# A three-block fp32 network on one core: the end of a stage and the start of the next run by token tile

## What is computed

```python
for i in range(2):                      # blocks 0 and 1
    g = norm_g[i]
    h = h + 0.5 * rmsnorm(swiglu(rmsnorm(h, g[0]), wg1[i], wu1[i], wd1[i]), g[1])
    u = rmsnorm(h, g[2])
    m = diff_attention(u) if i == 0 else neighborhood_attention(u)   # w_in 1024x3072, w_out 1024x1024
    h = h + rmsnorm(m, g[3])
    h = h + 0.5 * rmsnorm(swiglu(rmsnorm(h, g[4]), wg2[i], wu2[i], wd2[i]), g[5])
def swiglu(x, wg, wu, wd):              # wg, wu 1024x2816, wd 2816x1024
    return (silu(x @ wg) * (x @ wu)) @ wd
# third block
p = rmsnorm(h, ga) @ w_in               # two attentions of 8 heads, forget logits, 2048 gate columns
h = h + (gates[0] * (o_a @ w_branch_moba) + gates[1] * (o_b @ w_branch_fox)) @ w_out
u, g = split(rmsnorm(h, gf) @ w_ffn_up)
out = h + (silu(causal_conv3(g)) * u) @ w_ffn_down
```

## Time and profile before

| | before |
|---|---|
| median of 3 runs | 1442.16 us (1442.08 to 1443.78) |
| the profiled execution | 1442.12 us, span 1440.3 us |
| PE busy | 1422.6 us |
| DVE, ACT, POOL busy | 858.5, 747.9, 90.9 us |
| granted PE clock, whole span | 1.00 |
| transfers | 248.21 MB, mean 172 GB/s |

### The profile page before, as it was taken

One profiled execution on the slowest core, in us unless ns is written; L12 is line 12 of the kernel. 1 busy time (PEld: TensorE's weight loads), 2 busy tenths in 40 slices (PEclk: granted clock), 3 DMA queues, 4 the chain that ended last, 5 costly groups with the idle time before them and its releaser, 6 DMA issues.

```text
span 1440.3 us, 20791 instructions
## 1 busy us (share of the span) xinstructions
PE 1422.6 (99%) x6864; PEld 1184.1 (82%) x6864; DVE 858.5 (60%) x1113; ACT 747.9 (52%) x1216; POOL 90.9 (6%) x115
## 2 busy tenths in 40 slices
PE   9999999999999999999999999999999999999999
PEld 7888888778888888888888988888888898888887
DVE  5555575767555565555655665555657756565654
ACT  6444464656444454444546654444545465465553
POOL 2110110012111000000100000000013000000000
PEclk9999999999999999999999999999999999999999
DMA  9877746315655656556463155566565513555551
GB/s 304 245 224 219 219 155 210 118 59 160 190 189 189 203 162 190 189 187 195 157 219 111 37 160 189 188 187 201 181 208 161 176 60 104 178 167 181 184 183 53
DMA packets 189938, 248.21 MB, mean 172 GB/s; under 512 B 15194, under 2 KB 128101, under 8 KB 189760
## 3 DMA queue, kind: packets, MB, share of 16 engines
q1 hardware_dynamic: 187904, 241.35, 53.1%
q0 software_dynamic: 1984, 6.21, 1.9%
HBM read 246.33 MB, written 1.17 MB: 172 GB/s over the span
## 4 chain that ended last, share of the span: by engine, by line
PE 93%; DVE 3%; ACT 1%; issue 1%; POOL 1%; DMA 0%; SPq 0%; ACTq 0%; DVEq 0%; POOLq 0%
PE ps L272 26%; PE ps L274 26%; PE ps L273 26%; PE ps L760 2%; PE ps L796 2%; PE ps L555 1%; PE ps L785 1%; PE ps L285 1%; DVE h L476 1%; PE ps L367 1%; PE ps L962 1%; PE ps L286 1%; PE ps L290 1%; PE ps L332 1%; PE ps L331 1%
## 5 line engine op out<-in xcount | busy, mean ns | idle before, releaser
L265 DVE TENSOR_TENSOR wlo<-raw,whi 128x1024 fp32r<-128x1024 f32 x450 | 549.5, 1230 | 393.4 <-ACT whi L257 393.2
L257 ACT CAST whi<-raw 128x1024 fp32r<-128x1024 f32 x450 | 469.9, 1051 | 361.5 <-PE ps L274 344.9
L272 PE MATMUL ps<-whi,xhi 128*128 128x512 f32 x1280 | 499.9, 391 | 0.0
L274 PE MATMUL ps<-whi,xlo 128*128 128x512 f32 x1280 | 498.2, 389 | 0.0
L273 PE MATMUL ps<-wlo,xhi 128*128 128x512 f32 x1280 | 498.0, 389 | 0.0
L274 PEld LDWEIGHTS ps<-whi,xlo 128*128 128x128 f32 x1280 | 240.2, 188 | 50.3
L272 PEld LDWEIGHTS ps<-whi,xhi 128*128 128x128 f32 x1280 | 240.3, 188 | 49.5
L273 PEld LDWEIGHTS ps<-wlo,xhi 128*128 128x128 f32 x1280 | 240.3, 188 | 49.3
L272 PE MATMUL ps<-whi,thi 128*128 128x512 f32 x400 | 160.5, 401 | 0.0
L274 PE MATMUL ps<-whi,tlo 128*128 128x512 f32 x400 | 156.4, 391 | 0.0
L273 PE MATMUL ps<-wlo,thi 128*128 128x512 f32 x400 | 156.0, 390 | 0.0
(11 more groups left out here) (181 smaller groups left out, 1141.2 us busy)
## 6 DMA issues: line engine op xcount, KB each, us to landing
raw<-in_ffn_wg_dram SPq DMA_DIRECT2D x176, 256.0 KB, 2.9
raw<-in_ffn_wu_dram SPq DMA_DIRECT2D x176, 256.0 KB, 3.1
raw<-in_ffn_wd_dram SPq DMA_DIRECT2D x176, 256.0 KB, 3.0
raw<-in_w_ffn_up_dram SPq DMA_DIRECT2D x88, 256.0 KB, 3.5
raw<-in_w_in_dram SPq DMA_DIRECT2D x80, 256.0 KB, 3.3
raw<-in_diff_w_in_dram SPq DMA_DIRECT2D x48, 256.0 KB, 3.0
raw<-in_na_w_in_dram SPq DMA_DIRECT2D x48, 256.0 KB, 3.1
raw<-in_w_ffn_down_dram SPq DMA_DIRECT2D x44, 256.0 KB, 3.0
```

Of the source, the lines that this page charges most:

```text
L257: nc.scalar.copy(whi[:, s], raw[:, s]).then_inc(s_hi, 1)
L265: nc.vector.tensor_tensor(wlo[:, s], raw[:, s], whi[:, s].bitcast(F32), ALU.subtract).then_inc(s_lo, 1)
L272: nc.tensor.matmul(outs[t], ahi[:, c], whi[:, s, i], start=start, stop=False)
L274: last = nc.tensor.matmul(outs[t], alo[:, c], whi[:, s, i], start=False, stop=stop)
```

## The change

Three things. **The end:** the last three units of f0 to f3, out0 and out1 (the last two of out2) run through `held_rows`, all tile-0 products of the held units first, then tile 1; ahead of the last unit's tile-1 products stand the first four transposes of the next stage. The turned hidden of an FFN's last chunk goes to `xhi`/`xlo` (k 6 and 7), so that it doesn't wait for unit n0+63. The end of f4 stays as it was. **The start:** `first_chunk` works the first four units of the next stage as tile 0 rounded products, tile 0 residual products (`xlo`), tile 1, with the other twelve transposes of h between them, four at a time; `keep_warm` is gone there. ACT and DVE split the turned h in pieces of 128 x 128 (`split_act`, `split_dve`), 16 on each instead of 8 of 128 x 256. The chunk writes banks Y and Y+1. **The kernel's start** has the same form, with x in three transfers between the units, and the gains on ACT's queue.

```diff
+        def rounded_part(pe, n0, r, j, t):
+            s, c, o = slot(n0 + j), slice(t * P, (t + 1) * P), ps[:, Y + t]
+            pe.wait_ge(s_hi, n0 + j + 1)
+            pe.wait_ge(s_xh, XB[r] + 4 * t + j + 1)
+            for i in range(2):
+                nc.tensor.matmul(o, xhi[:, 2 * j + i, c], whi[:, s, i], start=j == 0 and i == 0, stop=False)
+            pe.wait_ge(s_lo, RING + n0 + j + 1)
+            for i in range(2):
+                nc.tensor.matmul(o, xhi[:, 2 * j + i, c], wlo[:, s, i], start=False, stop=False)
...
+        def turn_half(pe, r, t, b):
+            if r == 0:
+                pe.wait_ge(s_x[2 if t else b], 16)
+            else:
+                pe.wait_ge(s_src, 4 * (r - 1) + 2 * t + b + 1)
+            if t:
+                pe.wait_ge(s_xl, XB[r] + 2 * b + 2)
+            for k in range(4):
+                ins = nc.tensor.transpose(turned(t, 4 * b + k), h[:, t, (4 * b + k) * P:(4 * b + k + 1) * P], ident)
+            ins.then_inc(s_tr, 1)
+
+        def first_chunk(pe, n0, r, mid=None):
+            rounded_part(pe, n0, r, 0, 0)
+            turn_half(pe, r, 0, 1)
+            for j in range(1, UP):
+                rounded_part(pe, n0, r, j, 0)
+            turn_half(pe, r, 1, 0)
+            if mid is not None:
+                mid()
+            rest_part(pe, n0, r, 0, 0)
+            rest_part(pe, n0, r, 1, 0)
+            turn_half(pe, r, 1, 1)
+            rest_part(pe, n0, r, 2, 0)
+            rest_part(pe, n0, r, 3, 0)
+            for j in range(UP):
+                rounded_part(pe, n0, r, j, 1)
+                rest_part(pe, n0, r, j, 1).then_inc(s_used, 1)
+
+        def held_rows(pe, units, base, r):
+            for t in range(NT):
+                c = slice(t * P, (t + 1) * P)
+                for u, (n0, ahi, alo, ready) in enumerate(units):
+                    if t == 0:
+                        pe.wait_ge(s_lo, RING + n0 + 1)
+                        if ready is not None:
+                            pe.wait_ge(*ready)
+                    elif u == len(units) - 1:
+                        turn_half(pe, r, 0, 0)
...
+        def next_act(act, r, gain, q, last):
+            split_act(act, r, gain, 0, 1)
+            pre_act(act, q, 0)
+            for b in range(2):
+                split_act(act, r, gain, 1, b)
+            hi(act, last - 1 + RING)
+            pre_act(act, q, 1)
+            hi(act, last + RING)
+
+        def post_act(act, q, yt, last, factor, r, gain, nq):
             for idx in range(4):
                 t, i = idx // 2, idx % 2
+                if idx == 2:
+                    hi(act, last - 2 + RING)
+                    split_act(act, r, gain, 0, 0)
                 y_bank(act, yt, last, idx)
...
+        def next_dve(dve, r, gain, last):
+            split_dve(dve, r, gain, 0, 1)
+            for b in range(2):
+                split_dve(dve, r, gain, 1, b)
+            for j in range(2):
+                lo(dve, last - 1 + j + RING)
...
+                if t == 0:
+                    lo(dve, last - 2 + RING)
+                    split_dve(dve, r, gain, 0, 0)
+            next_dve(dve, r, gain, last)
...
+                gate_up(pe, n0 + 4, NCH - 2)
+                pe.wait_ge(s_htl, b + 2 * NCH - 2)
+                row_unit(pe, n0 + 8, NCH - 2, thi[:, 0], tlo[:, 0], Y, False, False)
+                turn(NCH - 1)
+                held_rows(pe, [(n0 + 63, thi[:, 1], tlo[:, 1], None)] +
+                          [(n0 + 64 + j, thiB[:, j], tloB[:, j], (s_htl, b + 2 * NCH - 1 + j)) for j in range(2)], Y, nr)
+                return
...
+            sp.dma_start(h[:, 0, 0:512], x[0, 0:P, 0:512]).then_inc(s_x[0], 16)
+            def load_x(j):
+                if j == 0:
+                    sp.dma_start(h[:, 0, 512:D], x[0, 0:P, 512:D]).then_inc(s_x[1], 16)
+                if j == 3:
+                    sp.dma_start(h[:, 1], x[0, P:S, :]).then_inc(s_x[2], 16)
+            ffn_sp(sp, n["f0"], *ffn_w[0], 0, load_x)
```

More of the change, by code:

```diff
@@ L46 @@
 NAP = 16
+SPLIT = (0, 1, 3, 4, 5, 7, 8, 11)
+XB = [sum(8 if q in SPLIT else 4 for q in range(r)) for r in range(12)]
 C_ID, C_ROPE, C_WIN, C_CAUS, C_TRI, C_FLIP, C_HEAD, C_END = 0, 128, 192, 256, 384, 896, 1024, 1032
@@ L155, in build @@
         s_yt = sem("y_bank_done")
-        s_x = [sem(f"x_landed{t}") for t in range(NT)]
+        s_x = [sem(f"x_landed{i}") for i in range(3)]
         s_rows = sem("rows_landed")
@@ new lines, in rest_part, with turned @@
+        def rest_part(pe, n0, r, j, t):
+            s, c, o = slot(n0 + j), slice(t * P, (t + 1) * P), ps[:, Y + t]
+            pe.wait_ge(s_xl, XB[r] + 4 * t + j + 1)
+            for i in range(2):
+                last = nc.tensor.matmul(o, xlo[:, 2 * j + i, c], whi[:, s, i], start=False, stop=j == UP - 1 and i == 1)
+            return last
+        def turned(t, k):
+            return ps[:, Z + k // 2, (k % 2) * S + t * P:(k % 2) * S + (t + 1) * P]
+        def turn_half(pe, r, t, b):
[8 more added lines that the diff above has]
+            ins.then_inc(s_tr, 1)
@@ new lines, in held_rows @@
+        def held_rows(pe, units, base, r):
[8 more added lines that the diff above has]
+                        turn_half(pe, r, 0, 0)
+                    s, end = slot(n0), u == len(units) - 1
+                    for i in range(2):
+                        o = ps[:, base + 2 * t + i]
+                        nc.tensor.matmul(o, ahi[:, c], whi[:, s, i], start=False, stop=False)
+                        nc.tensor.matmul(o, ahi[:, c], wlo[:, s, i], start=False, stop=False)
+                        last = nc.tensor.matmul(o, alo[:, c], whi[:, s, i], start=False, stop=end)
+                        if end and (t == 0 or i == 0):
+                            last.then_inc(s_yt, 1)
+                    if t == 1:
+                        last.then_inc(s_used, 1)
@@ L296, in col_unit @@
+        def col_unit(pe, n0, it, j, banks):
             s = slot(n0)
             pe.wait_ge(s_lo, RING + n0 + 1 + RING * it)
[L298 to L302, removed]
             for i in range(2):
```

263 lines of the change are left out of this document (140 added, 123 removed).

## The result

The change runs in 1433.18 us (median of 4 runs, 1432.91 to 1434.73) against 1442.68 us for the kernel before on the same chip (1442.08 to 1443.78): a ratio of 0.9937, with an interval of 0.9925 to 0.9950. The prediction was 1431, with 1426 to 1437.5 as its range. The profiled executions are 1433.22 us (span 1431.4) against 1442.12 (span 1440.3), so 8.9 us have gone, where the sum had 11.3.

What follows compares the result with a forecast made beforehand. PE, 99% busy, bounds the kernel, with 30.4 us of product-free gaps at seven stage ends. Gaining 13.2 there less 1.9 at the start gives 11.3 off 1442.12: 1430.8, said as 1431, range 1426 to 1437.5.

Steps and rivals of the forecast that it cites:

- the sum: Whole kernel: 13.2 us gained at seven stage ends less 1.9 lost at the kernel's start, 11.3 us, giving 1430.8.
- The gap: Stage ends: 4.45 us without products at six places, 3.70 at out2; the 16 transposes, 1.8 us, stay on PE.
- The hidden residual: Ends of f0 to f3: PE waits for the second hidden residual behind a weight subtraction on DVE, 0.6 us with restart.
- The first transposes: Stage ends: h is ready 3.11 us after the last tile-0 product starts, products cover 2.95; wait with restart 0.24 us.
- The products that wait for splits: Next stage's first chunk: rounded tile-0 products of units 2 and 3 wait 0.1 us for the second split.
- Transposes of tile 1 and all weights covered: Behind stage ends: no wait for tile 1's h, by 0.3 us at least, nor for later units' weights, by 1.9 or more.
- the rival of pieces at 0.49: Splits at seven ends and the start: pieces take 0.49 us, not 0.28, costing 12 us, 1443; chance 0.14 for all between.
- The start: Kernel's start: PE stands until unit 3's residual weights at 15.3; the chunk ends at 24.1 instead of 22.2, loss 1.9 us.
- the rival (0.08): Kernel's start: PE, working half of the time, runs at half speed; 16 products cost 3.4 us more, 1434; chance 0.08.
- The free start: Kernel's start: costs nothing, since the order of loads helps more than estimated, 1429; chance 0.12.
- the dry ring: Stage boundaries: late weight casts make PE wait for unit n0+4; 5 us late costs 17 us, 1448; chance 0.04.

Runs made afterwards that it cites:

- the combination with warm-ups: The changed kernel with the old kernel start, both hidden casts ahead of the weight cast, and eight warm-ups behind the third attention: 1428.57 us, and 1428.52 when run again.

## Why the prediction was right, and where not

**The gap and what stays of it.** Right. At f0's end 84 products at 0.2274 us (19.10), four fours of transposes (1.8) and those of the hidden (0.45) leave 22.34 - 21.35 = 0.99 us of waits, where the prediction had 0.94. Before, the same products and the hidden's transposes with the gap of 4.45 make 24.0, and 23.99 was read.

**The waits.** The hidden residual: predicted 0.6; the step from 193.06 to 193.79 and the restart behind it hold 0.58, and taking it away gave 0.52 to 0.59 at each of four places. The first transposes: predicted 0.24; 197.74 to 198.12 holds 0.15 beyond a step, 0.2 with the restart of the product behind them. The products that wait for splits: predicted 0.1; two pairs from 201.82 to 202.87 take 1.05 instead of 0.91, 0.14, and the rest of the 0.99, under 0.1, is spread. Transposes of tile 1 and all weights covered, as said: none is in PE's waits behind the start. The kernel with two held units shows that what covers the wait for h is the products that stand ahead of it.

**The pieces.** Four take 1.12 to 1.14 us on either engine, 0.28 each: the value taken from other operations of that shape was right, and the rival of pieces at 0.49 is out.

**The start.** Right in sign and mechanism, too small: 2.47 us instead of 1.9 in the profiled execution, and 2.1 to 3.7 over the six profiled executions with this start and these loads. The upper two are a later landing (3.29) and a fall of the clock (3.67), as read above. The step that failed is "DVE alone (four subtractions, eight pieces from about 7.8) gives 15.0". DVE began at 8.69, since its first work is a subtraction behind ACT's four pieces and its cast, and it then stood 0.39 us for unit 1: 15.87. I had taken the landing and DVE's own work as two limits of which the later counts, and left ACT out; here the three are in series. The loss that the sum lacked, 0.57 us, is just 15.87 against the 15.3 that it took. Behind 15.87 the estimate was good: 8.9 us to the fifth unit's first product, where 8.8 was said. (Before, that product starts at 22.30 and not at 22.2: 27.75 less 24 products; this changes the loss by under 0.1.)

**The clock.** A fall was in no term of the sum: it took full speed everywhere, from stretches of one trace that all showed 1.00, and the rival (0.08) was about the start alone. In part that 1.00 was misread. In the first 6 to 10 us of a span the 1.00 means that the trace has no entry of the clock there, not that the clock was full (the last section has the rows); so the start does begin at half speed, before the change as well as behind it. The twelve profiles of the change and its variants show that a stretch's clock is not a property of the kernel. Behind the third attention PE stands for the same 1.02 us in all nine profiles without warm-ups there, the kernel before among them; the clock fell in two of these (the change's first, and the one with the old loads) and stayed up in the change's second. At the start it fell in two of the seven profiles of kernels with the new form there. The rival's price at the start was 3.4 us; the kernel with two held units lost 1.2 us to its fall there, the one with the old loads 1.7. The Trainium skill (TensorE: Matmul & The Clock Gate, "The HAM clock gate") says that idleness brings the slow clock back; the rows agree in that each fall while PE still had work stands behind a wait of PE. That rule alone does not decide, since the same wait of 1.02 us passed at 1.00 in seven of nine profiles. Why the change falls more often than the kernel before (five of its eight runs are under 1.000, three of them at 0.997; of the 22 runs of the kernel before in the three groups four are, all at 0.999) is open, for only a few of the runs have a profile.

**The rivals.** The free start is out, the dry ring is out (PE's waits name a weight only in the kernel's start), wide pieces are out. The slow start happened in part, in some executions. Of the 2.4 us between the sum and the first profile of the change 1.65 are the fall; the second profile, without one, took 1431.76, against 1430.8 by the sum.

## What to carry to other kernels

When an engine shows 99% busy, look at what it does between the last and the first product of two stages; work that must wait for a norm can be covered by the other tile's products, but only if both sides of the border are reordered, and here a unit held was worth its products' time, as long as the wait was open. Add up what stands in series at a kernel's start, landing, cast, subtraction, and keep there the order that needs the fewest units. What the clock does behind a wait of a microsecond one trace doesn't tell: ask several executions before you count on it. Warm-up matmuls there have a price that a trace shows, 0.6 us here; what they save needs more profiled runs than these.

## What was unexpected of the hardware

The granted clock of one and the same stretch differed between executions. For the same instructions and the same wait of 1.02 us ahead of them, eight transposes took 1.81 us at 0.50 and 1.09 at 1.00, and the clock was back at 1.00 after 3.4 us. At the start of the kernel with the old loads it stayed down for 10 us.

The first transposes of x took 0.21 us each instead of 0.11, although the granted clock is shown as 1.00 there. The trace settles this. Its entries of the granted clock begin only at 8.56 us in the kernel before, and a stretch without an entry is shown as 1.00. PE's steps change from 0.21 to 0.11 us at that moment: of the kernel before, two windows, with 6 and 12 instructions on PE.

```profile
7.00:8.00 1.00, 1.00 (x6) 1.00 (x5) 0.00 (x0) 0.00 (x0) 0.00 (x0) 1.00 1.07 373
9.00:10.00 1.00, 1.00 (x12) 1.00 (x11) 0.03 (x1) 1.00 (x2) 0.00 (x0) 1.00 0.91 335
```

All twelve profiles that have such entries agree: the first lies between 5.7 and 10.0 us, and the step halves there. So the first transposes ran at half speed (1.2 GHz). In the kernel with the old start PE did nothing but the 16 transposes of x from 6.34 to 9.81 us, behind ten warm-ups and the turn of the gains up to 5.4, and the clock rose at 9.97. The rule of the Trainium skill that the prediction cites (TensorE: Matmul & The Clock Gate, "PE-mode transpose"), by which transposes don't count as activity, is hard to square with these rows.

The landing of unit 0, with the old start's loads, varied so that its cast began at 8.78 us in one profiled execution of the combination with warm-ups and at 9.90 in another; the two took 1427.83 and 1429.01, and the landing accounts for the difference between them.
